# Expert gate-and-up weights in two transfers of 4 MB with 32 KB runs, in place of four of 2 MB with 16 KB runs

## What is computed

```python
logits = hf @ w_router + b_router            # 256 tokens, 32 experts
top_val, top_idx = lax.top_k(logits, 4)
gate = softmax(top_val)
for e in range(32):                          # tokens routed to e
    gu = xb @ w_gu[e] + b_gu[e]              # w_gu[e]: 1024 x 2048
    g, u = gu[:, :1024], gu[:, 1024:]
    g, u = minimum(g, 7), clip(u, -7, 7)
    y = ((u + 1) * (g * sigmoid(1.702 * g))) @ w_down[e] + b_down[e]   # w_down[e]: 1024 x 1024
    out[tokens] += y * gate
```

## Time and profile before

| | |
|---|---|
| median of three runs | 1315.12 us (1314.77 to 1315.67) |
| the profiled execution, its own time | 1316.92 us |
| span of its instructions | 1315.2 us |
| TensorE matmul busy | 1239.3 us (94%) |
| DMA moved | 454.67 MB, mean 346 GB/s |
| mean granted TensorE clock | 0.993 |

### The profile page before, as it was taken

One profiled execution on the slowest core, in us unless ns is written; L12 is line 12 of the kernel. 1 busy time (PEld: TensorE's weight loads), 2 busy tenths in 40 slices (PEclk: granted clock), 3 DMA queues, 4 the chain that ended last, 5 costly groups with the idle time before them and its releaser, 6 DMA issues.

```text
span 1315.2 us, 14804 instructions
## 1 busy us (share of the span) xinstructions
PE 1239.3 (94%) x6149; PEld 608.0 (46%) x6149; DVE 284.6 (22%) x695; ACT 147.6 (11%) x329; POOL 7.1 (1%) x34
## 2 busy tenths in 40 slices
PE   6999999999999999999999988999999899999986
PEld 5858886667744334333433333333333334333322
DVE  1262334321132122111211111122111121221111
ACT  2213322101310000000000000000000000000001
POOL 1000000000000000000000000000000000000000
PEclk9989999999989999999999999999999999999999
DMA  9951332447547999899999999999999999999996
GB/s 329 311 193 64 129 117 76 159 175 281 200 192 305 428 428 428 335 422 428 428 429 428 429 429 429 428 428 429 429 429 428 428 428 428 428 426 427 429 428 267
DMA packets 60433, 454.67 MB, mean 346 GB/s; under 512 B 7212, under 2 KB 14056, under 8 KB 35048
## 3 DMA queue, kind: packets, MB, share of 16 engines
q1 hardware_dynamic: 58008, 451.96, 83.8%
q10 hardware_dynamic: 2384, 2.11, 0.5%
HBM read 453.00 MB, written 1.05 MB: 345 GB/s over the span
## 4 chain that ended last, share of the span: by engine, by line
PE 63%; DMA 32%; DVE 2%; SPq 1%; issue 1%; ACT 0%; DVEq 0%; ACTq 0%
DMA r_odd<-in_w_gu_dram 30%; PE ps L1286 26%; PE ps L876 14%; PE ps L883 7%; PE ps L1263 3%; PE ps L1279 3%; DMA ring<-in_w_down_dram 2%; PE ps L1360 2%; SPq L489 1%; PE ps L1063 1%; PE ps L1385 1%; PE ps L1380 1%; PE ps L865 1%; PE ps L1247 1%; DMA r_x<-in_x_dram 0%
## 5 line engine op out<-in xcount | busy, mean ns | idle before, releaser
L1286 PE MATMUL ps<-ring,r_memT 128*64 128x512 f32 x1024 | 227.9, 595 | 23.9 <-DMA ring<-in_w_gu_dram 23.1
L1286 PE MATMUL ps<-r_odd,r_memT 128*64 128x512 f32 x1024 | 227.1, 594 | 24.4 <-DMA r_odd<-in_w_gu_dram 24.4
L1286 PE MATMUL ps<-ring,r_kx 128*64 128x512 f32 x768 | 171.1, 594 | 0.4 <-DMA ring<-in_w_down_dram 0.4
L1943 DVE TENSOR_SCALAR r_ga<-ps 128x512 f32<-128x512 f32 x32 | 22.1, 691 | 676.0 <-PE ps L1286 676.0
L1286 PEld LDWEIGHTS ps<-r_odd,r_memT 128*64 128x64 f32 x1024 | 71.8, 137 | 177.0 <-issue 128.3
L1286 PEld LDWEIGHTS ps<-ring,r_memT 128*64 128x64 f32 x1024 | 71.0, 137 | 175.8 <-issue 129.1
L876 PE MATMUL ps<-r_odd,ring 128*128 128x256 f32 x640 | 143.8, 384 | 0.0
L876 PEld LDWEIGHTS ps<-r_odd,ring 128*128 128x128 f32 x640 | 121.9, 192 | 19.7 <-issue 3.3
L1286 PEld LDWEIGHTS ps<-ring,r_kx 128*64 128x64 f32 x768 | 54.4, 137 | 113.8 <-issue 107.7
L817 ACT ACTIVATE r_ga<-r_ga 128x512 f32<-128x512 f32 x32 | 20.1, 630 | 516.8 <-DVE r_ga L1943 516.8
L1263 PE MATMUL ps<-r_dm,r_x 128*128 128x128 f32 x512 | 65.8, 283 | 0.0
(11 more groups left out here) (333 smaller groups left out, 771.7 us busy)
## 6 DMA issues: line engine op xcount, KB each, us to landing
ring<-in_w_gu_dram SPq DMA_DIRECT2D x64, 2048.0 KB, 28.9
r_odd<-in_w_gu_dram SPq DMA_DIRECT2D x60, 2048.0 KB, 31.3
ring<-in_w_down_dram SPq DMA_DIRECT2D x47, 2048.0 KB, 22.6
r_gbx<-in_w_down_dram SPq DMA_DIRECT2D x15, 2048.0 KB, 44.5
ring<-in_w_in_dram SPq DMA_DIRECT2D x8, 2048.0 KB, 13.2
r_odd<-in_w_gu_dram SPq DMA_DIRECT2D x8, 1024.0 KB, 12.5
ring<-in_w_k_x_dram SPq DMA_DIRECT2D x2, 2048.0 KB, 9.4
ring<-in_w_v_x_dram SPq DMA_DIRECT2D x2, 2048.0 KB, 8.2
```

Source lines behind the costliest of these rows:

```text
L1286: last = mm(ps[n * SLOTS:(n + 1) * SLOTS, bk, :], stationary_, moving(n), start=start, stop=stop, skip_group_check=True)
L1943: V.tensor_scalar(gact, ps[:, GBK, :], 7.0, None, ALU.min).then_inc(g_limited, 1)
```

## The change

The four tensors of the odd slots become one, `r_odds`, so that slots 0 and 1, and 2 and 3, lie next to each other in every partition; in `ring` the slots of `gu0`/`gu1` and of `gu2`/`gu3` do so already. `gu_dram` now gives partition p four neighbouring rows (32 KB in HBM) of one of two groups q, and `gu_part(e, j)` is half of such a group. `even_pair` and `odd_pair` load two slots in one transfer of 4 MB. They wait until the second slot of the two is free, and raise the semaphore of the first. TensorE waits for the pair ahead of its first piece; what it waits for ahead of the second has been met since the start. TensorE signals a slot free once for each pair. `x_rows` and `gain2` follow the new order: the step between the gathered columns is four elements, in place of two. Expert 0, expert 1, and `gu2` and `gu3` of the last expert are still loaded in pieces of 2 MB or 1 MB. The load of `gfin` waits for `odd_freed[3]`, in place of `odd_freed[2]`. The loads of w_down are unchanged.

```diff
-        r_odd = [sb(f"r_odd{j}", [P, SLOT_W]) for j in range(4)]
+        r_odds = sb("r_odds", [P, 4, SLOT_W])
+        r_odd = [r_odds[:, j] for j in range(4)]
...
-        x_rows = r_x[:].rearrange("p (t j q k) -> p t j k q", t=TT, j=4, k=2)
+        x_rows = r_x[:].rearrange("p (t q r k) -> p t q k r", t=TT, q=2, k=4)
...
-        gu_dram = A["w_gu"].rearrange("l e (j p k) n -> (l e) j p k n", k=2, p=P)
+        gu_dram = A["w_gu"].rearrange("l e (q p k) n -> (l e) q p k n", k=4, p=P)
...
+            def gu_part(e, j):
+                return gu_dram[e, j // 2][:, 2 * (j % 2):2 * (j % 2) + 2]
+
+            def even_pair(e, q):
+                s = eslot[EXPERT_PIECES[2 * q]]
+                assert eslot[EXPERT_PIECES[2 * q + 1]] == s + 1
+                dst = ring[:, s:s + 2].rearrange("p s (k n) -> p (s k) n", k=2)
+                sp.dma_start(dst, gu_dram[e, q]).then_inc(loaded[s], 16)
+
+            def odd_pair(e, q):
+                dst = r_odds[:, 2 * q:2 * q + 2].rearrange("p s (k n) -> p (s k) n", k=2)
+                sp.dma_start(dst, gu_dram[e, q]).then_inc(odd_loaded[2 * q], 16)
...
             def odd_heads(p):
 
-                for j in range(HEADS):
-                    sp.wait_ge(odd_freed[j], p)
-                    odd_piece(p * 2 + 1, j)
+                for q in range(2):
+                    sp.wait_ge(odd_freed[2 * q + 1], p)
+                    odd_pair(p * 2 + 1, q)
+                sp.wait_ge(odd_freed[4], p)
+                odd_piece(p * 2 + 1, 4)
 
             def even_heads(p):
 
-                for j in range(HEADS):
-                    sp.wait_ge(freed[eslot[EXPERT_PIECES[j]]], p)
-                    expert_piece(p * 2, j)
+                for q in range(2):
+                    sp.wait_ge(freed[eslot[EXPERT_PIECES[2 * q + 1]]], p)
+                    even_pair(p * 2, q)
+                sp.wait_ge(freed[eslot["dn0"]], p)
+                expert_piece(p * 2, 4)
...
-            for j in range(HEADS):
-                sp.wait_ge(odd_freed[j], NE // 2 - 1)
-                if j < 3:
-                    odd_piece(NE - 1, j)
-            in_halves(odd_slot[3], gu_dram[NE - 1, 3], 2, odd_loaded[3], rest_loaded[0])
+            sp.wait_ge(odd_freed[1], NE // 2 - 1)
+            odd_pair(NE - 1, 0)
+            sp.wait_ge(odd_freed[3], NE // 2 - 1)
+            odd_piece(NE - 1, 2)
+            in_halves(odd_slot[3], gu_part(NE - 1, 3), 2, odd_loaded[3], rest_loaded[0])
+            sp.wait_ge(odd_freed[4], NE // 2 - 1)
             in_halves(odd_slot[4], dn_dram[NE - 1, 0], 4, odd_loaded[4], rest_loaded[1])
...
-            sp.wait_ge(odd_freed[2], NE // 2)
+            sp.wait_ge(odd_freed[3], NE // 2)
...
-            def piece_rows(j, uses, odd):
-
+            def piece_rows(j, uses, odd, last_expert=False):
+
+                second = j in (1, 3)
                 if odd and j < HEADS:
-                    pe.wait_ge(odd_loaded[j], uses * 16 + (32 if j < 3 else 16))
+                    if not second:
+                        pe.wait_ge(odd_loaded[j], uses * 16 + (32 if j < 3 else 16))
+                    elif j == 3 and last_expert:
+                        pe.wait_ge(odd_loaded[3], 32)
+                    else:
+                        pe.wait_ge(odd_loaded[j], 32 if j == 1 else 16)
                     return lambda k, a: odd_slot[j][:, k, a:a + 512]
                 s = eslot[EXPERT_PIECES[j]]
-                pe.wait_ge(loaded[s], uses * 16 + (16 * dmas[s] + 16))
+                pe.wait_ge(loaded[s], (0 if second else uses * 16) + (16 * dmas[s] + 16))
...
-                    last.then_inc(odd_freed[j] if odd and j < HEADS else freed[eslot[EXPERT_PIECES[j]]], 1)
+                    if j % 2:
+                        last.then_inc(odd_freed[j] if odd else freed[eslot[EXPERT_PIECES[j]]], 1)
```

More of the change, by code:

```diff
@@ L474, in expert_piece @@
                 if j < 4:
-                    dst, src = ring[:, s].rearrange("p (k n) -> p k n", k=2), gu_dram[e, j]
+                    dst, src = ring[:, s].rearrange("p (k n) -> p k n", k=2), gu_part(e, j)
                 else:
@@ L485, in odd_half @@
             def odd_half(e, j, k):
-                sp.dma_start(odd_slot[j][:, k], gu_dram[e, j][:, k]).then_inc(odd_loaded[j], 16)
+                sp.dma_start(odd_slot[j][:, k], gu_part(e, j)[:, k]).then_inc(odd_loaded[j], 16)
             def odd_piece(e, j):
-                sp.dma_start(odd_slot[j], gu_dram[e, j] if j < 4 else dn_dram[e, j - 4]).then_inc(odd_loaded[j], 16)
+                sp.dma_start(odd_slot[j], gu_part(e, j) if j < 4 else dn_dram[e, j - 4]).then_inc(odd_loaded[j], 16)
             def odd_heads(p):
-                for j in range(HEADS):
-                    sp.wait_ge(odd_freed[j], p)
-                    odd_piece(p * 2 + 1, j)
-            def even_heads(p):
-                for j in range(HEADS):
-                    sp.wait_ge(freed[eslot[EXPERT_PIECES[j]]], p)
-                    expert_piece(p * 2, j)
+                for q in range(2):
[3 more added lines that the diff above has]
+                odd_piece(p * 2 + 1, 4)
+            def even_heads(p):
+                for q in range(2):
[3 more added lines that the diff above has]
+                expert_piece(p * 2, 4)
             def others(i):
@@ L561, in _ @@
                     e = sp.value_load(cnt_i[0:1, bass.ds(i - (NE - 1), 1)], min_val=0, max_val=NE - 1)
-                    for j in range(6):
+                    for q in range(2):
+                        sp.wait_ge(freed[eslot[EXPERT_PIECES[2 * q + 1]]], i - NE // 2)
+                        even_pair(e, q)
+                    for j in (4, 5):
                         sp.wait_ge(freed[eslot[EXPERT_PIECES[j]]], i - NE // 2 if j < HEADS else i)
@@ L767, in _ @@
                     .then_inc(late_loaded, 16)
-            act.dma_start(gain2.rearrange("p (j k) -> p j k", k=2), A["g_ffn"][0].rearrange("(j p k) -> p j k", p=P, k=2))\
+            act.dma_start(gain2.rearrange("p (q k) -> p q k", k=4), A["g_ffn"][0].rearrange("(q p k) -> p q k", p=P, k=4))\
                 .then_inc(late_loaded, 16)
@@ L1262, in gather_half @@
                     for t in range(TT):
-                        last = mm(ps[:, buf, c * P:(c + 1) * P], x_rows[:, t, 2 * q + c // 2, c % 2],
+                        last = mm(ps[:, buf, c * P:(c + 1) * P], x_rows[:, t, q, c],
                                   place[:, t], start=(t == 0), stop=(t == 1))
@@ L1270, in gather_late @@
                     for t in range(TT):
-                        last = mm(ps[:, XBK, c * SLOTS:(c + 1) * SLOTS], x_rows[:, t, c // 2, c % 2],
+                        last = mm(ps[:, XBK, c * SLOTS:(c + 1) * SLOTS], x_rows[:, t, c // 4, c % 4],
                                   place[:, t, 0:SLOTS], start=(t == 0), stop=(t == 1))
@@ L1367, in gate_up @@
                         pe.wait_ge(xg_ready, 1 + j // 2)
-                    w = piece_rows(j, heads_used if j < HEADS else i, odd)
+                    w = piece_rows(j, heads_used if j < HEADS else i, odd, is_block(i, NE - 1))
                     for k in range(2):
```

## The result

| | before | after |
|---|---|---|
| median of the runs | 1314.94 us (1311.03 to 1316.97, 6 runs) | 1325.89 us (1323.93 to 1327.50, 6 runs) |
| ratio, 95% interval | | 1.0086 (1.0070 to 1.0103) |
| profiled execution, its own time | 1316.92 us | 1324.18 us |
| span | 1315.2 us | 1322.3 us |
| TensorE matmul busy | 1239.3 us | 1286.0 us |

A forecast was written before the change was run, and what follows sets the result against it. The prediction took the experts to be bound by DMA. Its terms, 3.4 + 0.1 + 2.1 - 4.7 = +0.9 us on 1315.12, gave 1316.0 us, range 1312.3 to 1319.9.

The forecast's parts named there:

- What bounds the kernel: Experts: DMA-bound, 29.4 us of DMA each against about 26.4 us of TensorE, whose busy share hides it.
- The gap hangs on a landing: Stream gap near 553 us: depends on dn1 of expert 5 landing, so it moves whole with the stream ahead.
- (5): Gather's weight loads at step four: 11 ns more each, 0.2 us an expert, hidden; counted 0.1 us, ends 0 and 0.35.
- (1): Stream start: the first pair, for expert 2, waits one TensorE piece longer, so the stream starts 3.4 us later.
- (2): DMA rate with 32 KB runs: saves 0.080 us a pair, 4.7 us over 59 pairs.
- (3): Last expert: gu0 and gu1 land as one pair, leaving TensorE four pieces; gate-up ends 2.1 us later.
- (4): Steady part: each expert ends 3.5 us later against the stream, but 14.2 us of queued loads keep engines fed; nothing lost.
- (6): Final gain's load: issued after gu3, some 1296.8 us, there by 1309.1, wanted at about 1311; costs nothing.
- The sum without (5): Whole kernel: 3.4 + 2.1 - 4.7 = +0.8 us against before.
- That the rate might not move: Rival, DMA stream: saving below 0.051 us a pair, time 1317.8 to 1320.7 us; chance 0.24.
- The clock: Rival, longer TensorE waits: clock falls, losing some 1.7 us each, showing only in the last expert, 1316.9 us; chance 0.12.
- The dry queue: Rival, DMA queue: runs dry if TensorE comes over 14 us late each expert; 1325 us or more; chance 0.03.

The follow-up runs named there:

- m1: Kernel before, with a step of one element in the gather's weight loads and in the transposes of the hidden values; 1316.46 us, one run.
- m3: Kernel before, with a step of three elements in the gather and two in the transposes of the hidden values; 1321.66 us, one run.
- e2: Changed kernel with the gather's old step of two elements, all pairs and 32 KB runs kept; 1317.03 us, ratio 1.0026.
- e3: Kernel before, with 4 MB pairs and their waits, but two 16 KB runs per partition and the old gather step; 1320.40 us, ratio 1.0054.
- e5: Changed kernel with gather step two, and gu0 to gu3 of expert 2 and gu0, gu1 of expert 31 in 2 MB loads; 1310.62 us, ratio 0.9966.
- f1: Changed kernel with ScalarE copying tokens into gather order, and 2 MB loads for gu0 to gu3 of expert 2 and gu0, gu1 of expert 31; 1313.04 us.
- f3: f1 with gu2 and gu3 of expert 30 in single 2 MB loads too; 1310.05 us, ratio 0.9962.
- f2: Changed kernel with only ScalarE's copy of the tokens into the gather's order added; 1316.22 us, ratio 1.0005.
- e1: Kernel before, 2 MB loads and old waits, with only the new order of rows and the gather's step of four; 1328.82 us, ratio 1.0110.
- e4: Changed kernel with gu0 to gu3 of expert 2 and gu0, gu1 of expert 31 in 2 MB loads; 1326.25 us, run a second time 1326.24 us.

## Why the prediction was wrong, point by point

**What bounds the kernel: right, but used only half.** The DMA bound in the steady part, the gap that hangs on `dn1` of expert 5 and the last waits all stood in the traces as read. But I drew from "DMA-bound" that TensorE's time is hidden. It is hidden only behind the restart. The six experts ahead of it are on the path: their length, not the landing, can set when SyncE may go on. "The gap hangs on a landing" was true by 0.38 us, the wait at 553.41, and I never asked by how much.

**(5), the gather: the step that failed.** It said 11 ns a load, from the earlier trace rows, 0.2 us an expert, hidden. Measured: 328 ns in place of 197, 1.84 us an expert, 10.5 us up to the restart and 3.7 in the double gather ahead of it. Both the price and the overlap ("under the DMA's 29.4") were wrong. Two mistakes stand in it. The first: the 208 ns of L1385 are those of a transpose, whose load takes 141 ns when contiguous (m1), and I compared it with a matmul's load that takes 193. The rows for that were in the trace of before: L1380 has transposes from contiguous data.

```profile
L1385 PEld LDWEIGHTS ps<-ident,r_kx 128*128 128x128 f32 x128 | 17.8, 204 | 1.7 <-DVE r_kx L1951 1.7
L1380 PEld LDWEIGHTS ps<-ident,r_dm 128*128 128x128 f32 x64 | 6.4, 141 | 25.2 <-issue 25.2
```

Beside them the strided transpose was 45% dearer, no small direction. And m3 shows that even the right pair would not have given the size, as the two forms follow different curves. The second: its ends, 0 and 0.35 us, came from the same comparison and not from asking what it costs if that is wrong. The Trainium skill (Advanced Engine Details and Errata, Memory Cachelines) asks for two accesses in one 16-byte line and names a penalty for a new line each time; the gather agrees with it to the step: 198 ns at two elements in a line, 261 at 1.33, 328 at one. The transposes do not agree with it: at a step of two, with two elements in a line, they already take 210 ns in place of 141. I cited it as speaking against this edit, and gave it no chance of its own.

**(1), the later start: right in mechanism, and hidden here.** In e2 and e3, where TensorE is quick, it costs what was said: e2's restart, at 560.76, is 161.5 us behind its first expert, 2.5 more than before, where 3.4 less 0.8 was forecast for the landing. e3 reaches the last landing of expert 30 at 1260.21 us, 866.8 us behind its first expert at 393.43, 2.6 us more than before, where 3.4 less 0.5 was worked out:

```profile
393.43 13.91 PE ps L1311 x64
```

```profile
1260.21 8.52 PE L1311 MATMUL ps<-ring,r_memT 128*64 128x512 f32 x32 [2.61 <-DMA ring<-in_w_gu_dram]
```

In the changed kernel the restart waits for TensorE, and the term vanished under the larger one.

**(2), the rate: right.** 430 GB/s in 570 to 1250 us, and 0.080 us a pair (e5), the value taken between two extrapolations from shorter runs. But not all of it is the length of the runs, as (2) had it. e3 has pairs with the old 16 KB runs, and up to the last landing of expert 30 it is 2.6 us later than before, where the later start alone makes 3.4: the 58 pairs saved 0.8 us, some 0.013 each, as fewer transfers. e2 reaches that landing 4.2 us before e3, both counted from their first experts: 0.072 a pair for the length.

**(3), the tail: right for the changed kernel; where TensorE is quick another path, and 2.6 us in place of 2.1.** In the changed kernel TensorE waited 1.27 us for the last pair and then ran all four pieces, as forecast:

```profile
1287.77 13.95 PE L1307 MATMUL ps<-r_odds,r_memT 128*64 128x512 f32 x64 [1.27 <-DMA r_odds<-in_w_gu_dram]
```

In e2 and e3 it does not wait for the last pair at all (nor for the last single loads in e5 and f1). It comes late from expert 30, where it waited for a whole pair and then took 1.4 to 1.7 us longer for the matmuls; the cover that the prediction called just enough did not reach. f3 shows it: single loads there bring 2.4 us.

**(4), the queue: right.** The DMA share stays at 1.00 from 570 to 1250 us in e2 as in the changed kernel, though each expert ends later against the stream. Between 1000 and 1062 us `dn1` lands 17.5 and 19.0 us after its issue in e2, where 19 was forecast.

**(6), the final gain: right;** no kernel waited for it.

**The sum without (5)** was +0.8. Measured: e2 +2.3 (ratio 1.0026, 1.0015 to 1.0036), f2 +1.2 (1.0005, 0.9993 to 1.0017).

**The rivals.** That the rate might not move fell. The clock did fall behind the long waits, at the price given (8.78 - 7.09 = 1.7 us), and it ate up no queue; that it could reach the end of the kernel was seen for the last expert, but not that expert 30 is enough, and that single loads in expert 31 alone would then bring little. The dry queue's number, 1325 or more, was met by luck: behind the restart the queue never ran dry. No rival had the gather as its mechanism. That was the gap in the list: a term with an unchecked price of near zero is a rival too.

## What to carry to other kernels

A layout that makes DMA runs longer sets the step with which other engines read the matching operand; price that read first, on the same instruction form, since here it cost about 1% (e1) where the pairs brought 4.5 us, 0.3% (e5). In a kernel that is bound by DMA later on, TensorE's time ahead of the last restart of the stream can still count almost in full; read how long TensorE waits for the last landing there (here 0.38 us), since that is all the cover it has. Longer transfers can pay in the middle of a saturated stream while single ones are kept at its start, at its end, and in the last block in which a long wait would drop the clock on the way out: f3 has both, and is 0.4% faster than before.

## What the runs showed of the hardware that I had not expected

The weight load of a 128 x 128 fp32 matmul: 193, 198, 261, 328, 335 ns at a step of one, two, three, four and eight elements, and that of a transpose 141 ns contiguous and 210 and 208 in the median at a step of two and four. The matmuls of the gather go along: 16 of them take 1.88 us at 198 ns a load and 3.73 us at 328.

The time at which experts start differs between profiles by up to 9 us (393.4 in e3's, 402.4 in e4's second). 3.4 us of that are e4's longer gather; the rest comes from two places where the clock falls in some executions and not in others. One is at about 384 us, behind short waits for VectorE: the granted clock from 384 to 392 us is 0.52 and then 0.50 before, 0.82 and then 1.00 after. These are the four residual matmuls ahead of the gather, in the chains of the kernel before and after:

```profile
390.04 3.57 PE ps L1247 x4
```

```profile
386.46 1.80 PE ps L1268 x4
```

The same instructions take half as long where the granted clock had come back. The other place is at about 80 us, where the granted clock of 60 to 120 us is 0.94 in the profile before and 1.00 in the one after. The chains show 16 of the same matmuls there, before and after:

```profile
79.78 8.56 PE ps L883 x16
```

```profile
80.54 6.87 PE ps L904 x16
```

By 112 us the kernel before is 2.6 us behind, and it stays so until 376 us. Over the runs the mean granted clock and the time go together: of the kernel before beside e1, those at 0.998 took 1310.8 to 1311.6 us, those at 0.994 to 0.996 took 1314.4 to 1315.6. So these falls probably make most of the spread of some 5 us within each kernel's runs (only the profiled ones show where they lie), and they are why the ledgers above count from the first expert.

A wait of some 2.5 us for a pair was followed by matmuls 1.4 to 1.7 us longer often, but not always, in e2, e5 and f1 (mean granted clock 0.982 to 0.983): in e2's timeline between 640 and 1262 us behind 8 of 11 such waits. The wait that follows a fall is about as much shorter (0.8 to 1.1 us), and behind it there was none; so the loss does not add up. Behind the waits of 0.70 us in the changed kernel there was no fall (0.998).
